# One core, attention layer: ScalarE splits the projection weights, GpSimd rotates two pairs, the convolution's layer norm moves into the first attention items

## The reference

```python
for l in range(2):
    x = x + 0.5 * swiglu(rms_norm(x, ffn1_norm[l]), ...)
    h = rms_norm(x, mix_norm[l])
    (a_val, a_gate, b_gate, c_gate, b_h, q, k, v,
     q_idx, k_idx, w_idx) = split(h @ w_in[l])
    # GLU -> causal depthwise conv (31 taps, 256 channels) -> LayerNorm over the channels -> silu
    y_a = silu(layer_norm(causal_dwconv(a_val * sigmoid(a_gate), dw) + dw_b))
    # gated convolution with 3 taps, 256 channels
    y_b = b_gate * causal_dwconv(c_gate * b_h, sc_dw)
    q, k, q_idx, k_idx = rotary(...)
    # per token the 128 best causal keys by the indexer's score, then attention over them, 8 heads of 64
    y_c = dsa_attention(q, k, v, q_idx, k_idx, w_idx)
    x = x + concat([y_a, y_b, y_c]) @ w_out[l]
    x = x + memory_cross_attention(...)
    x = x + 0.5 * swiglu(rms_norm(x, ffn2_norm[l]), ...)
```

## Time and profile before

| | |
|---|---|
| median of 3 runs | 4051.4 us (4032.7 to 4058.5) |
| the profiled execution | 4037.83 us |
| its span in the trace | 4036.0 us, mean granted clock 0.938 |
| busy | PE 92%, PEld 75%, DVE 51%, ACT 23%, POOL 51% |
| first layer: ACT starts to evict tile 7 / the v products end / the attention goes on | 465.92 / 589.62 / 618.34 us |
| second layer: the same | 1709.10 / 1826.97 / 1852.20 us |
| ACT's last `h_hi` of the attention | 710.81 and 1936.55 us |

### The profile page before, as it was taken

The page is one execution under the profiler, slowest core; times in us unless marked ns, Lnnn a source line. Parts: engine busy times, 40 slices in busy tenths (PEclk is TensorE's granted clock), DMA queues, the critical chain, the costliest instruction groups (busy, mean ns, idle before and its releaser), DMA issues.

```text
span 4036.0 us, 44417 instructions
## 1 busy us (share of the span) xinstructions
PE 3703.0 (92%) x16816; PEld 3008.2 (75%) x16816; DVE 2066.6 (51%) x3105; ACT 913.2 (23%) x1583; POOL 2045.3 (51%) x1215
## 2 busy tenths in 40 slices
PE   6999968989999999987989998978899989789998
PEld 5888746778888888765778886756788767578877
DVE  5542776645533552596635532363666225446651
ACT  2110225231111110115332111123223112232320
POOL 4666551436666666561336664611466654116664
PEclk9999987999999999998999999967899989689999
DMA  3333360313333233262313332301133332102332
GB/s 113 99 95 99 96 148 16 121 52 96 98 94 101 94 99 96 85 147 53 110 59 98 95 95 85 109 27 32 58 94 99 87 113 69 32 16 94 98 88 86
DMA packets 102637, 347.62 MB, mean 86 GB/s; under 512 B 13840, under 2 KB 14512, under 8 KB 101936
## 3 DMA queue, kind: packets, MB, share of 16 engines
q1 hardware_dynamic: 92080, 320.59, 25.9%
q0 software_dynamic: 4320, 15.73, 2.1%
q10 hardware_dynamic: 6048, 8.66, 0.8%
HBM read 318.45 MB, written 2.10 MB: 79 GB/s over the span
## 4 chain that ended last, share of the span: by engine, by line
PE 31%; DVE 12%; issue 5%; ACT 4%; DMA 1%; DVEq 0%; ACTq 0%; POOL 0%; POOLq 0%
PE banks L505 10%; PE banks L507 9%; PE banks L506 9%; DVE diagonals L811 3%; DVE squares L815 1%; DVE pair L1912 1%; ACT diagonals L780 1%; DVE scaled L819 1%; DVE diagonals L807 1%; ACT act_hi L788 1%; ACT squares L783 1%; PE banks L1618 1%; ACT probs L870 0%; DVE h_lo L660 0%; DMA w_raw<-mid 0%
## 5 line engine op out<-in xcount | busy, mean ns | idle before, releaser
L528 POOL CAST w_hi<-w_raw 128x1024 fp32r<-128x1024 f32 (+1 forms) x602 | 670.2, 1113 | 1873.2 <-PE banks L507 1696.0
L533 POOL TENSOR_TENSOR w_lo<-w_raw,w_hi 128x1024 fp32r<-128x1024 f32 (+1 forms) x540 | 1310.3, 2426 | 43.3
L505 PE MATMUL banks<-h_hi,w_hi 128*128 128x512 f32 x2944 | 1170.2, 398 | 73.7 <-DVE h_lo L1442 19.8
L506 PE MATMUL banks<-h_lo,w_hi 128*128 128x512 f32 x2944 | 1155.4, 392 | 0.0
L507 PE MATMUL banks<-h_hi,w_lo 128*128 128x512 f32 x2944 | 1155.1, 392 | 0.0
L505 PEld LDWEIGHTS banks<-h_hi,w_hi 128*128 128x128 f32 x2944 | 557.9, 189 | 219.0 <-issue 59.9
L507 PEld LDWEIGHTS banks<-h_hi,w_lo 128*128 128x128 f32 x2944 | 558.2, 190 | 118.2
L506 PEld LDWEIGHTS banks<-h_lo,w_hi 128*128 128x128 f32 x2944 | 559.0, 190 | 110.8
L505 PE MATMUL banks<-act_hi,w_hi 128*128 128x512 f32 x1056 | 412.7, 391 | 8.5 <-DVE act_lo L821 8.5
L506 PE MATMUL banks<-act_lo,w_hi 128*128 128x512 f32 x1056 | 412.5, 391 | 0.0
L507 PE MATMUL banks<-act_hi,w_lo 128*128 128x512 f32 x1056 | 412.2, 390 | 0.0
(11 more groups left out here) (358 smaller groups left out, 4436.5 us busy)
## 6 DMA issues: line engine op xcount, KB each, us to landing
w_raw<-gu SPq DMA_DIRECT2D x176, 512.0 KB, 3.5
w_raw<-mid SPq DMA_DIRECT2D x130, 512.0 KB, 3.5
w_raw<-up SPq DMA_DIRECT2D x88, 512.0 KB, 3.5
w_raw<-dn SPq DMA_DIRECT2D x96, 448.0 KB, 3.3
w_raw<-mix SPq DMA_DIRECT2D x64, 512.0 KB, 3.5
w_raw<-dn SPq DMA_DIRECT2D x48, 512.0 KB, 3.5
w_lo<-w_raw POOLq DMA_DIRECT2D x30, 512.0 KB, 5.5
qk_swap<-qk_raw ACTq DMA_DIRECT2D x64, 64.0 KB, 4.6
```

The costliest lines, as they stand in the source:

```text
L505: pe.matmul(out, w_hi, m_hi, start=start, stop=False, skip_group_check=True)
L506: pe.matmul(out, w_hi, m_lo, start=False, stop=False, skip_group_check=True)
L528: g.tensor_copy(wh[:, ch.slot, 0:width], raw[:, ch.raw, 0:width]).then_inc(Ring.hi[ch.slot], 1)
L533: eng.tensor_tensor(wl[:, ch.slot, 0:width], raw[:, ch.raw, 0:width], f32(wh[:, ch.slot, 0:width]), ALU.subtract).then_inc(Ring.split[ch.s ...
```

## The change

Four things change.

- `ADDED` begins at chunk 10. For all 18 of its chunks ACT writes the high part too (`split_hi_minus`), straight after `evict(j)` and its DMAs, so POOL has no CAST in this stretch, only the DMA that adds. The split of chunk 27 moves behind the four `v_hi`.
- The tiles 7 to 20 come in another order: k3 q4 c0 h0 k5 c1 h1 q6 b0 b1 k7 q8 k9 q10. ACT scales q by -1/8 when it evicts.
- POOL rotates the pairs 3 to 6 (`pool_rope`, 20 instructions), in between the chunks' DMAs. The short convolution is in another order, and its six tap products go to ACT (`short_taps`).
- The layer norm's steps are spread over the attention's steps 1 to 7. `out_part` starts at `s = 8`, two quarters at each of two steps, then one or two steps without (`part_at`).

```diff
-ADDED = {l * C1 + FFN_CHUNKS + m for l in range(L) for m in range(13, 28)}
+ADDED = {l * C1 + FFN_CHUNKS + m for l in range(L) for m in range(10, 28)}
...
-    def split_minus(act, ch):
-
+    def split_hi_minus(act, ch):
+
+        act.wait_ge(Ring.raw_in[ch.raw], 16 * (ch.n // RAWS + 1))
+        act.wait_ge(Ring.done, ch.n + 1)
+        act.activation(wh[:, ch.slot, 0:A], raw[:, ch.raw, 0:A], ACT.Copy).then_inc(Ring.hi[ch.slot], 1)
         act.wait_ge(Ring.hi[ch.slot], ch.turn)
         act.activation(wl[:, ch.slot, 0:A], f32(wh[:, ch.slot, 0:A]), ACT.Copy, scale=-1.0).then_inc(Ring.minus, 1)
...
     def split(g, ch, src, width):
-        split_hi(g, ch, width)
         if ch.added:
             split_add(g, ch)
         else:
+            split_hi(g, ch, width)
             split_lo(g, ch, width)
...
-    PART_FROM = 2
+    def part_at(d):
+
+        return 8 + 7 * d // 2
...
-        pe.wait_ge(v_lo_s.sem, v_lo_s(l, T))
-        pe.wait_ge(ln_inv.sem, ln_inv(l, 1))
...
+        def conv_norm(s):
+            if s == 1:
+                pe.wait_ge(conv1.sem, conv1(l, 2 * CONVW + 2))
+                for k in range(2):
+                    mm = pe.matmul(bank[2][:, :], ones[:, :], acc[:, k, :], start=(k == 0), stop=(k == 1))
+                mm.then_inc(ln_mean.sem, 1)
+            elif s == 2:
+                for k in range(2):
+                    pe.wait_ge(ln_sq.sem, ln_sq(l, k + 1))
+                    mm = pe.matmul(bank[3][:, :], ones[:, :], dev_sq[:, k, :], start=(k == 0), stop=(k == 1))
+                mm.then_inc(ln_var.sem, 1)
+            elif s == 4:
+                pe.wait_ge(ln_inv.sem, ln_inv(l, 1))
...
+    def short_taps(k):
...
-        for m in range(V_CHUNK + 3, OUT_CHUNK + 3):
-            minus(m)
+        for m in range(V_CHUNK + 3, OUT_CHUNK + 2):
+            own_split(m)
         products_done(act, mid_chunk(l, V_CHUNK + 3))
         for t in range(T):
             act.activation(v_hi[:, t, :], bank[4 + t][:, :], ACT.Copy, scale=st[:, 2, t:t + 1]).then_inc(v_hi_s.sem, 1)
+        own_split(OUT_CHUNK + 2)
...
+        def conv_norm(s):
+            if s == 3:
+                v.wait_ge(ln_var.sem, ln_var(l, 1))
+                v.tensor_scalar(ln_tmp[:, 0, :], bank[3][:, :], 1.0 / 256, 1e-5, ALU.mult, ALU.add)\
+                    .then_inc(ln_inv.sem, 1)
+            elif s == 5:
+                v.wait_ge(ln_rstd.sem, ln_rstd(l, 2))
+                refine_root(v, ln_tmp[:, 2, :], ln_tmp[:, 0, :], ln_tmp[:, 1, :], ln_inv.sem, ln_inv(l, 1))
+                for k in range(2):
+                    v.tensor_tensor(dev[:, k, :], dev[:, k, :], ln_tmp[:, 2, :], ALU.mult).then_inc(ln_y.sem, 1)
+            elif s == 7:
+                for k in range(2):
+                    yab_low(2 + k, k)
```

More of the change, by code:

```diff
@@ L884, in attention_act @@
                 emit_y(h)
+            if between is not None:
+                between(s)
     def attention_dve(v, a, l, score_banks, bias_of, key_tiles, t_hi, t_lo, emit_y, first=None, between=None):
@@ L989, in mix1_pe @@
         norm_pe_spread(pe, mixnorm, l)
-        for j in range(GLU_TILE, SHORT_TILE):
+        for j in range(GLU_TILE, AFTER_GLU):
             tile(j)
@@ L1004, in mix1_pe @@
                 ix_lo[r, 2, 0:n], True, True).then_inc(logit.sem, 1)
-        for j in range(SHORT_TILE, V_CHUNK):
+        for j in range(AFTER_GLU, V_CHUNK):
             tile(j)
@@ L1066, in out_part, with beside @@
                 mm.then_inc(part1.sem, 1)
-        attention_pe(pe, dsa, l, scores, SCORE_BANKS, dsa.max, causal_tiles, outputs, dsa.y_lo, out_part)
+        def beside(s):
+            conv_norm(s)
+            for d in range(KD):
+                if s in (part_at(d), part_at(d) + 1):
+                    for e in range(2):
+                        out_part(d, 2 * (s - part_at(d)) + e)
+        attention_pe(pe, dsa, l, scores, SCORE_BANKS, dsa.max, causal_tiles, outputs, dsa.y_lo, beside)
         pe.wait_ge(dsa.y_lo.sem, dsa.y_lo(l, HEADS))
@@ new lines, in beside_top_k @@
+    def beside_top_k(g, l, m):
+        if m == 10:
+            for i in range(4):
+                pool_rope(g, l, 3, i)
+        elif m == 11:
+            pool_rope(g, l, 3, 4)
+            for i in range(3):
+                pool_rope(g, l, 4, i)
+        elif m == 12:
+            for i in (3, 4):
+                pool_rope(g, l, 4, i)
+            short_rows(g, l)
+        elif m == 13:
+            short_in(g, l, 0)
+        elif m == 14:
+            for i in range(4):
+                pool_rope(g, l, 5, i)
+        elif m == 15:
+            pool_rope(g, l, 5, 4)
+            short_sum(g, l, 0)
+        elif m == 16:
+            short_in(g, l, 1)
+        elif m == 17:
+            for i in range(4):
+                pool_rope(g, l, 6, i)
+        elif m == 18:
+            pool_rope(g, l, 6, 4)
+            short_sum(g, l, 1)
+        elif m == 19:
+            for k in range(2):
+                short_out(g, l, k)
@@ L1262, in mix1_act @@
-        for k in range(2):
-            act.wait_ge(ya.sem, ya(l, k + 1))
-            act.activation(hh[:, k, :], acc[:, k, :], ACT.Copy).then_inc(yab_hi.sem, 1)
-        act.wait_ge(yab_lo.sem, yab_lo(l, 4))
+            act.activation(dev_sq[:, k, :], dev[:, k, :], ACT.Square).then_inc(ln_sq.sem, 1)
+        def conv_norm(s):
+            if s == 3:
+                act.wait_ge(ln_inv.sem, ln_inv(l, 1))
+                act.activation(ln_tmp[:, 1, :], ln_tmp[:, 0, :], ACT.Ln).then_inc(ln_rstd.sem, 1)
+                act.wait_ge(ln_rstd.sem, ln_rstd(l, 1))
+                act.activation(ln_tmp[:, 2, :], ln_tmp[:, 1, :], ACT.Exp, scale=-0.5).then_inc(ln_rstd.sem, 1)
+            elif s == 5:
+                for k in range(2):
+                    act.wait_ge(ln_y.sem, ln_y(l, k + 1))
+                    act.activation(dev[:, k, :], dev[:, k, :], ACT.Silu, bias=p1[:, l, LB0 + k:LB0 + k + 1],
+                                   scale=p1[:, l, LG0 + k:LG0 + k + 1]).then_inc(ya.sem, 1)
+                for k in range(2):
+                    act.wait_ge(ya.sem, ya(l, k + 1))
+                    act.activation(hh[:, k, :], dev[:, k, :], ACT.Copy).then_inc(yab_hi.sem, 1)
@@ L1461, in part_in, with ahead_of @@
             v.tensor_tensor(x[:, d, :], x[:, d, :], bank[7][:, :], ALU.add).then_inc(part1_x.sem, 1)
+        def ahead_of(s):
+            conv_norm(s)
+            for d in range(KD):
+                if s == part_at(d) + 2:
+                    part_in(d)
         def rope_in(s):
@@ L2040, in _ @@
             for l in range(L):
[L2041 removed]
+                stack1_chunks(g, l, split, split_hi_only, beside_top_k)
             for l in range(L):
```

238 lines of the change are left out of this document (116 added, 122 removed).

## The result

The changed kernel takes 3993.64 us (median of 4 runs, 3992.07 to 3996.87) against 4053.14 for the kernel before in the same comparison: ratio 0.9863, 95% interval 0.9829 to 0.9898. The 4053.14 is the median of only four runs that lie 26 us apart; over all 40 runs of before on record, on more than one chip (4019.47 to 4060.91), the median is 4042.0, and against that one the change brings some 48 us.

A forecast was written before the change was run, and what follows sets the result against it. The prediction saw PE gaps of some 24 and 18 us in the tiles, the largest ended by late adding DMAs. Tiles -14, POOL +18, attention -17 made -13: 4024.8 profiled, 4038 as median, range 4003 to 4070.

The forecast's parts named there:

- the attention: From the v products to the last h_hi: entry and rest together -14 and -3 us in the two layers, -17.
- the tiles: Tile 7's evict to the end of the v products: 6.5 us a tile, -10 and -4 us by layer.
- everything fits and PE sets the pace: Rival: without crowding a tile takes 5.9 us, 103 us a layer; under 4010, some 3998; chance 0.14.
- POOL beside the convolution: POOL's remaining rotations and short convolution risk being shut out by DVE's convolution, as the CASTs were: +18 us.
- POOL always gets in: Rival: groups behind a DMA issue get in between two of DVE's taps; gain 31 us, 4020; chance 0.25.
- The offset of 13.6 us: The median of the runs stands 13.6 us above the profiled execution; added to 4024.8 it gave 4038.
- the slots' loop: In the tiles: 20.6 us for three q or k tiles, 6.9 each, including ACT's 7.1 with four DMA issues.
- the raw buffers' loop: In the tiles: load, high and negative, issue, landing, 13.8 us for two chunks; 6.9 a chunk, or 5.9 if less crowded.
- The entry: From the v products to item 8's exp: 32 us in place of 48.1 and 44.3, 16 and 12 less.
- The rest of the attention: From item 8 to the last h_hi: 75 us in both layers, +2 and +10, for out_part's later matmuls.

The follow-up runs named there:

- e4: The changed kernel with the rotations of pairs 3 to 6 on DVE, right behind the convolution, instead of on POOL: 4004.77 us.
- e1: The changed kernel with the high part of chunks 10 to 27 as a CAST on POOL again: 4032.13 us.
- e7: The changed kernel with eight semaphore increments (0.6 us) on POOL between the adding DMA of chunks 17, 18, 19 and the tensor instructions behind it: 4004.33 us.
- e11: The changed kernel with the four swap DMAs of each q and k tile issued by SP instead of ACT: 4005.26 us.
- e12: The changed kernel with both the split of chunk 27 moved into the attention's step 4 and the swap DMAs issued by SP: 3996.84 us.
- e2: The kernel before, with only the high part of chunks 13 to 27 moved to ACT: 4014.33 us.
- e9: The changed kernel with ACT's split of chunk 27 moved from behind v_hi into the attention's step 4: 3984.38 us.
- e3: The changed kernel with the layer norm's steps ahead of the attention's first item, out_part unmoved: 3998.03 us.
- e10: The changed kernel with the norm ahead of the items and out_part one quarter a step from the second step, as before: 4014.83 us.
- e5: The kernel before, with POOL's CASTs of chunks 20 to 24 also waiting for given taps of the convolution: 4048.55 us, ratio 1.0005.
- e6: The kernel before, with POOL's CASTs of chunks 20 to 24 tied to given taps, then delayed 0.3 us by four semaphore increments: 4043.15 us, ratio 1.0011.

## Why the prediction was wrong

Of the 44.4 us between the 4038 forecast and the 3993.64 measured, 18 are the term for POOL, 12 the offset between the profiled execution and the median, 7 the attention, 5 the tiles, and 3 lie outside the stretches that I summed. The number itself is where my rival "everything fits and PE sets the pace" had it, under 4010 and some 3998, but not by that mechanism: it wanted tiles of 103 us, and they took 111.

**The step that failed is "POOL beside the convolution", +18.** It took the risk of the CASTs to move to the groups that stay on POOL, at one loss in two. None of after's groups was held in its traced execution, and its four runs lie 4.8 us apart, less than one held group costs. Over the traces of all fourteen kernels I counted POOL's instructions that begin during a tap of the convolution. Of those that begin 0.59 to 0.62 us after the start of a DMA issue, that is, by my reading, were in the queue behind it, 61 of 61 got in within 2 us; of those that follow another instruction of POOL within 0.5 us, 146 of 146. Of those that came to a POOL that had nothing to do (the lone ones, and the four at 0.77 and 1.01 us behind an issue), 20 of 31 were held, for 2.4 to 17.7 us; of the 11 that got in, five came 0.7 to 1.2 us after a tensor instruction of POOL, and none that came so was held. Every one of the 20 ended within 0.9 to 1.1 us of the start of the TENSOR_TENSOR with which DVE closes its run of taps (at 535.55 for the one of 17.73 us above), and none between two taps. So what decides is not the kind of instruction (TENSOR_TENSORs and CASTs were held) nor the point in the tap; the counts fit the reading that it is whether the instruction is already queued when the one before it ends. The trace has no record of the queue itself, and what makes 11 late ones get in and 20 not stays open. I had one pair behind an issue among the rows, named that reading in the rival "POOL always gets in", and gave it 0.25; I argued against it that a rotation waits for semaphores as a CAST does. In the code these semaphores are given well before, while the CAST waits for a DMA that lands at any time.

The page "SBUF — State Buffer" of the Trainium skill, section "Who interferes with whom", would have given the right sum, without the 18 us, by a wrong road. It says that issue order decides and not the shape of the op; that the kind of instruction doesn't decide, e4 and e1 bear out (a TENSOR_TENSOR of 11.22 us, a CAST of 12.43). But the pair isn't handed over at the end of one of DVE's instructions, neither in e7 (17.73 us) nor in before (12.61).

**The offset of 13.6 us** between the profiled execution and the median was the second error. I carried it over to after, whose median stands 1.6 us above its profiled execution. In before it was mostly the luck of three runs: over 40 runs the median is 4042.0, only 4.1 us above the profiled 4037.83, which has four held CASTs itself (9.79, 12.61, 3.07 and 11.04 us). So -45.8 in the profile became -59.5 against a before of four runs, and would be some -48 against all of them.

**The tiles**, -10 and -4: measured -12.4 and -6.4, the same within 2.4 us, from 6.5 us a tile and 3 for the start. That is in part luck. The reason that I gave for 6.5, the swaps' issues in the slots' loop, is refuted by e11 and e12 in their second layers (110.4 and 111.3 us). What sets the pace is then the raw buffers' loop (load, parts, landing); this is what is left of the two loops that I set up, and was not tried by itself. It is no fixed pace either: e2, with the same two raw buffers and the high part on ACT, takes 105.0 us in its second layer, 6.2 a tile.

**The price of the high part.** e2 alone brings 31 us, and without the high part on ACT (e1) the rest of the change brings 13; together 44 of some 48 to 60.

**The entry**, -16 and -12: measured -11.4 and -8.4. 3.7 us of the 4.6 missed in the first layer, and 2.3 of the 3.6 in the second, are ACT's wait for chunk 27, which e9 took away (first exp at 6.7, 7 expected); I had costed the two parts there and not the wait for their input. The gain itself has another cause than I gave. I credited it to the norm in the items; e3 shows that before item 8 the norm costs the same ahead of them. What pays is two other things. `v_hi` starts 0.1 and 0.4 us after the v products instead of 6.3 and 3.4, since the split of chunk 27 no longer stands ahead of it: 6.2 and 3.0 us. (e2, which keeps that order, still has 6.9 and 7.2.) This is the row of before ahead of `v_hi`:

```profile
595.00 1.06 ACT L539 ACTIVATE w_lo<-w_hi 128x1024 fp32r<-128x1024 f32 x1 [7.96 <-POOL w_hi L528]
```

And from `v_hi` to item 8 it takes 36.6 and 35.5 us instead of 41.8 and 40.9, for which `out_part`'s late start is the cause in the first layer: e10, with it from the second step, takes 43.0 and 38.4, against 36.0 and 36.6 in e3. In the second layer it gives 1.8 of the 5.4; the rest there stays open.

**The rest of the attention**, +2 and +10: measured -5.1 and +1.0. The windows from item 8 on (columns as above) have 310 matmuls in each layer, against 312 and 306 in the same windows of before:

```profile
613.01:681.01 68.00, 63.53 (x310) 48.14 (x309) 45.82 (x150) 40.41 (x108) 13.97 (x8) 0.96 0.10 28
1820.98:1887.27 66.29, 62.82 (x310) 47.92 (x310) 43.30 (x150) 40.40 (x107) 14.58 (x8) 0.97 0.10 32
```

I had said 18 more. Of `out_part`'s matmuls there are indeed more, 90 in each layer against 78 and 75, but of all others only 220 against 234 and 231: PE had that many more of the items' own matmuls behind it when ACT reached item 8. And the granted clock is higher in the first layer, 0.96 over this window against 0.90 in before, where it is low for the first 5 us and again from 667 to 677 us; in after it falls again too, but for 4 us. With `out_part` from the second step, the ten layers of before, e2, e5, e6 and e10 have a stretch of 103.4 to 106.3 us (four) or of 114.6 to 116.1 (six), and nothing between. In the six the clock stays at half until 46 to 48 us after the first `v_hi` and falls again at 70 to 72, for some 10 us; in the four it is back by 34 to 38 us and doesn't fall again. With it from the eighth step the clock is back by 29 to 36 us, later falls, up to 90 us, last 4 us at most, and none of the eighteen layers is over 104.6. Why the clock does the one in one layer and the other in the next stays open.

Each table load takes 1.28 us and the ACTIVATE begins at once (593.43 to 594.72), in after as in before; ahead of that load ACT was idle for 0.02 us. The 1380 ns of drain that the Trainium skill names in "ScalarE: Activation LUTs", section "What ACT_TABLE_LOAD costs", is not in these rows either.

## What to carry to other kernels

Where two engines hold each other up, as DVE and POOL here, look at what an instruction finds when it becomes ready, not only at its length: close behind a POOL instruction or a DMA issue it got in 207 times of 207 here, at an idle POOL it lost 20 times in 31, and everything queued behind it lost with it. So put what must get through beside a run of DVE instructions into one queue with no wait on late data in it, and give work that waits for a transfer to another engine. A kernel whose runs lie 40 us apart while its neighbour's lie 5 apart may be telling of such a draw, though runs that lie close don't rule a held instruction out (e1, e4 and e12 had them, with spreads of 7.3, 5.5 and 4.1 us). And before the offset between one profile and a median is carried over, take enough runs for the median: three of before were 9 us off.
